# Low-rank inputs of an RWKV-7/attention layer projected with the attention's keys and values (one core)

## The chip, the core and the metric

One core of a Trainium2 chip runs the whole program in one launch. The metric is device time in microseconds. Engines: TensorE (PE; its weight loads are the rows PEld), VectorE (DVE), ScalarE (ACT), GpSimd (POOL) and SyncE (SP, which here only issues DMAs). They run side by side and meet through semaphores; each goes through its own instructions in order.

## What is computed

One layer on x (2048 tokens, width 1024, float32). The part that matters:

```python
h = modulate(rms_norm(x, norm1_g), sh1, sc1)
proj = h @ w_in                       # columns: r 512, k 512, v 512, low rank 32+32+96, q 512, k 128, v 128
feat = proj[..., :RWKV_COLS]
feat = feat + (prev - feat) * shift_mix          # prev: the token before
r, k, v, w_lo, a_lo, g_lo = split(feat)
w = -softplus(-(w0 + tanh(w_lo) @ w2)) - 0.5     # decay
iclr = sigmoid(a0 + a_lo @ a2)
gate = sigmoid(g_lo) @ g2
# ... the recurrence over (r, decay, k, v, iclr), and beside it
# attention of q over a window of two chunks of 64 tokens, 8 query heads, 2 key/value heads
x = x + gt1 * (concat(y_rwkv, y_att) @ w_out)
x = x + gt2 * hier_moe(...)           # 32 experts, top 2
```

## The kernel before

**Passes.** The first pass (`pass1`) goes through 16 tiles of 128 tokens: input projection, all elementwise work of the RWKV group, and the windowed attention; it writes a pack per tile to memory. A second pass does the recurrence and the output projection, and then come the experts. Only the first pass is changed.

**Order.** Every engine runs the steps of one table, `ORDER`, in its order, each engine those it has a part in. An entry is a name and how many tiles ahead of the current one (t) it works: 0 is the current tile, 1 the next. The table is run once ahead of the loop with only the entries that work ahead, 15 times in full, and once with only the entries of the tile itself. So the projections of tile t+1 stand between the dependent steps of tile t on TensorE.

**Projection steps on TensorE.** `in_group` (matmuls on line 453) makes groups with channels as rows: 128 columns of w_in are the stationary operand, the transposed activations hT (128 tokens) the moving one, 8 matmuls per 128 channels. r, k and v have 4 times 128 channels, each group in two steps (in_r1, in_r2 and so on). The low-rank inputs are two more such pieces, `in_wa` (64 channels) and `in_g` (96 channels), 8 matmuls each. `in_tok` (line 464) makes groups with tokens as rows: hT is stationary and w_in moving, q with 512 columns in two steps of 4 matmuls (in_q1, in_q2), attention's keys and values with 256 columns in one step of 8 (in_kv).

**Other steps of TensorE, in order.** xT (L438) transposes the next tile's x; lora1 (L474, L479, L484) multiplies the low-rank inputs out; ew1 (L491), ew2 (L498), nbc (L504); att2 (L533) transposes normed q and k; att3_0 and att3_1 (L546) are the logits of heads 0 to 3 and 4 to 7; tok1 and tok2 (L516, L523) transpose RWKV features; att4_0 and att4_1 (L560) transpose the probabilities; att5_0 and att5_1 (L573) multiply them with the values.

**Steps on the other engines.** ev_r, ev_k, ev_v, ev_lora: ScalarE copies a group from PSUM (L618; for lora L615 and L616), GpSimd forms the difference to the token before (L720), VectorE mixes (L761). ev_q (L625) and ev_kv (L630) are ScalarE copies. xT on ScalarE (L602) modulates the next tile's activations into hT in 8 instructions. norm: ScalarE's squares (L593), then GpSimd and VectorE. tok1, tok2: ScalarE L663, VectorE L827. att2 on ScalarE: L673, L675. ew3 is VectorE's (L806 to L822). att3: VectorE adds the bias and finds the maximum (L840 to L851). exp_0 and exp_1: ScalarE's exponentials (L683). att4: ScalarE (L695) and VectorE (L861) each copy half of the transposed probabilities.

**PSUM banks.** `USES1` lists for each of the 8 banks its uses in a tile, in order; a use waits until the one before it was read. A0 holds r, v, q; A1 holds k, lora, kv; C3 holds three small things.

The table before, around the change:

```python
("ew3", 0), ("att3_0", 0), ("in_wa", 1),
("tok1", 0), ("exp_0", 0), ("in_g", 1), ("ev_v", 1), ("tok2", 0), ("att3_1", 0), ("exp_1", 0),
("in_q1", 1), ("att4_0", 0), ("in_q2", 1), ("att5_0", 0), ("ev_lora", 1), ("norm", 2),
("att4_1", 0), ("lora0", 1), ("in_kv", 1), ("ev_q", 1), ("att5_1", 0), ("out", 0), ("ev_kv", 1)
```

Of the kernel before, what the change touches and what calls it, by code (L numbers as in the profile page):

```python
# [21 lines left out]
ACT = mybir.ActivationFunctionType  # L22
# [4 lines left out]
P = 128  # L27
NT = T // P
KD = D // P
CHUNK = 64  # L30
HD = 64
C = 512
H = C // HD
CC = C // P
LORA_WA = 64
LORA_G = 96
RW_COLS = 3 * C + LORA_WA + LORA_G
QH, KVH = 8, 2
IN_COLS = RW_COLS + (QH + 2 * KVH) * HD
NF = 3 * CC + 2  # L40
LAMBDA = float(np.exp(-0.5))
NEG = -1e30
KEYS = 192
# [54 lines left out]
def shape_constants():  # L98
# [4 lines left out]
    def put(name, a):  # L103
# [32 lines left out]

USES1 = {"A0": ("r", "v", "q"), "A1": ("k", "lora", "kv"),
         "T0": ("xT", "qT", "tokA", "tokK", "P0", "P1"), "T1": ("xT", "kT", "tokB", "tokV", "P0", "P1"),  # L140
         "C0": ("zw", "nbc", "L0", "L1"), "C1": ("za", "L0", "L1"),
         "C2": ("gate",), "C3": ("ssn", "nT", "bon")}
BANK1 = {b: i for i, b in enumerate(USES1)}
IN_GROUPS = {"r": ("A0", 0), "k": ("A1", 1), "v": ("A0", 2), "lora": ("A1", 3)}


class Sync:
# [224 lines left out]
def pass1(nc, S, ps, V, W, ins, dram, nt):  # L372
    B = Banks(S, "a", USES1, nt, ahead=("xT", "r", "k", "v", "lora", "q", "kv"))
    bank = {b: ps[i] for b, i in BANK1.items()}
# [5 lines left out]
    ORDER = (("xT", 1), ("x", 2), ("lora1", 0), ("kk", 0), ("att1", 0), ("in_r1", 1), ("in_r2", 1), ("ew1", 0),  # L380
             ("in_k1", 1), ("ev_r", 1), ("ew2", 0), ("in_k2", 1), ("nbc", 0), ("att2", 0), ("in_v1", 1), ("in_v2", 1),
             ("ev_k", 1),
             ("ew3", 0), ("att3_0", 0), ("in_wa", 1),
             ("tok1", 0), ("exp_0", 0), ("in_g", 1), ("ev_v", 1), ("tok2", 0), ("att3_1", 0), ("exp_1", 0),
             ("in_q1", 1), ("att4_0", 0), ("in_q2", 1), ("att5_0", 0), ("ev_lora", 1), ("norm", 2),
             ("att4_1", 0), ("lora0", 1), ("in_kv", 1), ("ev_q", 1), ("att5_1", 0), ("out", 0), ("ev_kv", 1))

    def run(eng, steps):

# [11 lines left out]
    with nc.Block() as block:  # L401
        @block.sync
        def _(sp):
            def load_x(n, b):
                if isinstance(n, int) and n >= nt:
                    return
                B.wait_full(sp, "T1", "xT", n - 1)
                sp.dma_start(V["x"], dram["x"][bass.ds(n * P, P), :]).then_inc(S["x"], 16)

            def store(t, b):  # L410
                S.wait(sp, "ya", t + 1)
                sp.sem_inc(S["sp_passed"], 1)
                B.wait_read(sp, "T0", "tokK", t)
                sp.dma_start(dram["mid"][bass.ds(t, 1)].rearrange("a p n -> (a p) n"), V["pk_all"]).then_inc(S["stored"], 16)
                if isinstance(t, int) and t == nt - 2:

                    B.wait_full(sp, "A1", "kv", nt - 1)
                    sp.wait_ge(S["stored"], 16 * (nt - 1))
                    for n in range(2):
                        load_pack(sp, S, W, dram, n, n)  # L420
                    sp.dma_start(W["w_router"], ins["w_router"].rearrange("(k p) n -> p k n", p=P)).then_inc(S["w_out"], 16)
                    sp.dma_start(W["gt1"], ins["gate_b"][:, 0:D].to_broadcast([P, D])).then_inc(S["gate_b"], 16)

            sp.dma_start(dram["xn2"][T:T + 1, :].rearrange("o (a n) -> (o a) n", a=4),
                         V["S"][0:4, :]).then_inc(S["zero_row"], 16)
            run(sp, {"x": load_x, "out": store})
            sp.wait_ge(S["zero_row"], 16)
            sp.wait_ge(S["stored"], 16 * nt)

        @block.tensor  # L430
        def _(pe):
# [9 lines left out]
            def in_group(g, part):  # L441
                name, index = IN_GROUPS[g]

                def go(n, b):
                    if part == 0:
                        B.wait_read(pe, "T1", "xT", n)
                        B.wait_free(pe, name, g, n)
                    parts = [(P * c, P, C * index + P * c) for c in (2 * part, 2 * part + 1)]
                    if g == "lora":
                        parts = [[(0, LORA_WA, 3 * C)], [(P, LORA_G, 3 * C + LORA_WA)]][part]  # L450
                    for at, m, w0 in parts:
                        for kk in range(KD):
                            mm = pe.matmul(bank[name][0:m, at:at + P], V["w_in"][:, kk, w0:w0 + m], V["hT"][:, kk, :],  # L453
                                           start=(kk == 0), stop=(kk == KD - 1))
                    if part == 1:
                        B.full(mm, name)
                return go

            def in_tok(g, name, w0, w, ks=range(KD)):
                def go(n, b):  # L460
                    if ks[0] == 0:
                        B.wait_free(pe, name, g, n)
                    for kk in ks:
                        mm = pe.matmul(bank[name][:, 0:w], V["hT"][:, kk, :], V["w_in"][:, kk, w0:w0 + w],  # L464
                                       start=(kk == 0), stop=(kk == KD - 1))
                    if ks[-1] == KD - 1:
                        B.full(mm, name)
                return go

            def lora1(t, b):  # L470
                S.wait(pe, "lora_in", t + 1)
# [93 lines left out]
            def att5(g):  # L565
                def go(t, b):
                    B.wait_read(pe, "C2", "gate", t)
                    for i in range(4):
# [7 lines left out]
                return go  # L576

            run(pe, {"xT": xT, **{f"in_{g}{part + 1}": in_group(g, part) for g in "rkv" for part in range(2)},
                     "in_wa": in_group("lora", 0), "in_g": in_group("lora", 1),
                     "in_q1": in_tok("q", "A0", RW_COLS, C, range(0, 4)), "in_q2": in_tok("q", "A0", RW_COLS, C, range(4, KD)),  # L580
                     "in_kv": in_tok("kv", "A1", RW_COLS + C, 2 * P), "lora1": lora1, "ew1": ew1, "ew2": ew2, "nbc": nbc,
                     "tok1": tok((("tokA", "T0"), ("tokB", "T1"))), "tok2": tok((("tokK", "T0"), ("tokV", "T1"))),
                     "att2": att2, "att3_0": att3(0), "att3_1": att3(1), "att4_0": att4(0), "att4_1": att4(1),
                     "att5_0": att5(0), "att5_1": att5(1)})
# [2 lines left out]
        def _(act):  # L587
# [7 lines left out]
            def xT(n, b):  # L595
                for half, name in enumerate(("T0", "T1")):
                    B.wait_full(act, name, "xT", n)
                    if half == 0:
                        B.wait_full(act, "A1", "kv", n - 1)
                    for i in range(4):  # L600
                        c = 4 * half + i
                        a = act.activation(V["hT"][:, c, :], bank[name][:, P * i:P * i + P], ACT.Identity,  # L602
                                           scale=V["s1"][:, c:c + 1], bias=V["b1"][:, c:c + 1])
                        if i == 3:
                            B.free(a, name)

            def ev(g):
                name, index = IN_GROUPS[g]

                def go(n, b):  # L610
                    B.wait_full(act, name, g, n)
                    S.wait(act, "feat", 4 * (n - 1) + index + 1)
                    S.wait(act, "hist", 4 * (n - 1) + index + 1)
                    if g == "lora":
                        act.activation(V["raw_v"][0:LORA_WA, 12, 1:P + 1], bank[name][0:LORA_WA, 0:P], ACT.Copy)  # L615
                        a = act.activation(V["raw_v"][0:LORA_G, 13, 1:P + 1], bank[name][0:LORA_G, P:2 * P], ACT.Copy)  # L616
                    else:
                        a = act.activation(V["raw_v"][:, 4 * index:4 * index + 4, 1:P + 1],  # L618
                                           split(bank[name][:, :], 4), ACT.Copy)
                    B.free(a, name)  # L620
                return go

            def ev_q(n, b):
                B.wait_full(act, "A0", "q", n)
# [35 lines left out]
            def tok(use):  # L660
                def go(t, b):
                    B.wait_full(act, "T0", use, t)
                    B.free(act.activation(pk[use[3]], bank["T0"][:, :], ACT.Copy), "T0")  # L663
                return go
# [26 lines left out]
            def att4(g):  # L691
                def go(t, b):
# [3 lines left out]
                return go  # L696

            run(act, {"norm": norm, "xT": xT, "ev_r": ev("r"), "ev_k": ev("k"), "ev_v": ev("v"), "ev_lora": ev("lora"),
                      "ev_q": ev_q, "ev_kv": ev_kv, "lora0": lora1, "kk": kk, "ew1": ew1, "ew2": ew2, "tok1": tok("tokA"),
                      "tok2": tok("tokK"), "att1": att1,  # L700
                      "att2": att2, "exp_0": att3(0), "exp_1": att3(1), "att4_0": att4(0), "att4_1": att4(1)})

# [175 lines left out]
def views(nc, ctx):  # L878
# [3 lines left out]
    V = {}  # L882
# [22 lines left out]
    w_in_at = a.at  # L905
    V["w_in"] = split(a.take(KD * IN_COLS), KD)
    V["w_in_at"] = (w_in_at, a.at)
    for name, w in (("raw", NF * (P + 1)), ("qkv0", 768), ("qkv1", 768), ("Pb", 8 * 65), ("kT", 2 * KEYS), ("Pm", 1024)):
        V[name] = a.take(w)
    V["raw_v"], V["kT_v"], V["Pm_v"] = split(V["raw"], NF), split(V["kT"], 2), split(V["Pm"], 4)  # L910
    V["Pb_v"] = split(V["Pb"], 8)
# [1144 lines left out]
    return np.concatenate([up, down], 1).reshape(NE * PIECES, P, PIECE)  # L2056


def host_arrays(inputs):

    a = {n: np.asarray(v) for n, v in inputs.items()}
# [10 lines left out]
    for name, src in (("c", "c"), ("ada_b", "ada_b"), ("n1g", "norm1_g"), ("n2g", "norm2_g"), ("w0", "rwkv_w0"),  # L2072
# [5 lines left out]
    consts, onehot = shape_constants()  # L2078
    return {"x": a["x"].reshape(T, D), "cols": cols, "rows": rows, "consts": consts, "onehot": onehot,
            "gate_b": np.concatenate([b[2], b[5]])[None, :],  # L2080
            "ada": a["ada_w"][0].reshape(KD, P, 12, 512).transpose(2, 1, 0, 3).reshape(12, P, KD * 512), "w_in": a["w_in"][0], "w2": a["rwkv_w2"][0], "a2": a["rwkv_a2"][0],
            "g2": a["rwkv_g2"][0], "rel_bias": a["rel_bias"], "w_out": a["w_out"][0],
            "w_router": np.concatenate([a["router_grp_w"][0], a["router_exp_w"][0]], 1),
            "wex": expert_pieces(a["exp_w1"][0], a["exp_w3"][0], a["exp_w2"][0])}
# [13 lines left out]
```

## Time and profile before

| | |
|---|---|
| median of 3 runs | 2824.12 us (2823.98 to 2825.91) |
| the profiled execution | 2824.7 us, its span 2822.8 us |
| granted TensorE clock, mean | 0.937 of full |
| busy, share of the span | TensorE 88%, VectorE 38%, ScalarE 27%, GpSimd 15% |
| costliest group of the first pass | L453, TensorE matmuls, 3584 instructions, 419.2 us busy |
| the same for L464 | 512 instructions, 174.3 us busy |

The span runs from the first to the last instruction; the time beside it is the whole execution. Instructions of TensorE overlap, so a row's own length says more than the time it takes from the stream; that is read from start to start. A note in square brackets behind a row is idle time before it and what ended it.

### The profile page before, as it was taken

The page shows a single profiled execution, that of the slowest core. Times are in us where ns is not written, and L with a number is a line of the kernel's source. Part 1 is how long each engine was busy: PE and PEld are TensorE (multiplying, and loading weights), DVE is VectorE, ACT ScalarE, POOL GpSimd, SP SyncE. Part 2 cuts the span into 40 slices and gives each one's busy share as a digit, 9 for nine tenths or more (in the row PEclk, how much of TensorE's full clock was granted, in tenths as well). Part 3 has the DMA queues.
Part 4 walks back from the last instruction along what each step waited for, and adds up shares of the span by engine and source line. Part 5 has one row for each costly group of instructions (what it writes and reads, how often), then busy time and mean ns, then how long its engine had stood idle before and what let it go on. Part 6 is the DMA issues. An engine that isn't in the chain of part 4 may idle for free. (4 is left out here: it accounts for less than half of the span.)

```text
span 2822.8 us, 68456 instructions
## 1 busy us (share of the span) xinstructions
PE 2487.4 (88%) x28334; PEld 1608.1 (57%) x28335; DVE 1067.1 (38%) x2595; ACT 752.7 (27%) x1799; POOL 418.2 (15%) x497
## 2 busy tenths in 40 slices
PE   3999999999998789999999996479999999999940
PEld 2888888888887567777767674223332333232210
DVE  0344544544545245556555654411111111111108
ACT  0244344343343112232323231012222222221112
POOL 0212212212112012121212120000010101000000
PEclk8999999999998799999999997589999999999975
DMA  8012111111123732222222221565535396999959
GB/s 323 9 55 82 46 64 72 46 74 63 46 83 122 275 124 84 100 85 99 85 99 89 95 85 38 226 273 223 215 141 215 141 371 242 380 388 380 365 233 362
DMA packets 55113, 458.35 MB, mean 162 GB/s; under 512 B 7981, under 2 KB 9041, under 8 KB 32625
## 3 DMA queue, kind: packets, MB, share of 16 engines
q1 hardware_dynamic: 39240, 405.59, 36.7%
q0 software_dynamic: 10656, 38.80, 3.6%
q10 hardware_dynamic: 5000, 10.80, 1.1%
q8 instruction: 170, 2.79, 0.4%
q14 instruction: 47, 0.38, 0.0%
HBM read 367.61 MB, written 87.56 MB: 161 GB/s over the span
## 5 line engine op out<-in xcount | busy, mean ns | idle before, releaser
L1742 PE MATMUL ps<-arena 128*32 128x512 f32 x4608 | 513.4, 602 | 29.4 <-DMA arena<-wex 29.4
L453 PE MATMUL ps<-arena 128*128 128x128 f32 (+2 forms) x3584 | 419.2, 276 | 2.1 <-ACT arena L602 2.1
L453 PEld LDWEIGHTS ps<-arena 128*128 128x128 f32 (+2 forms) x3584 | 406.4, 186 | 16.9 <-ACT arena L602 12.9
L1742 PEld LDWEIGHTS ps<-arena 128*32 128x32 f32 x4608 | 150.4, 111 | 385.7 <-issue 362.7
L1100 PE MATMUL ps<-arena 64*64 64x64 f32 x8704 | 299.2, 222 | 30.0 <-ACT arena L1303 9.4
L1100 PEld LDWEIGHTS ps<-arena 64*64 64x64 f32 x8704 | 279.5, 137 | 58.4 <-issue 56.6
L1756 PE MATMUL ps<-arena 128*32 128x512 f32 x2304 | 267.3, 605 | 14.4 <-DMA arena<-wex 13.6
L1245 PE MATMUL ps<-arena 128*128 128x512 f32 x512 | 238.7, 610 | 0.7 <-ACT arena L1322 0.7
L1962 DVE TENSOR_TENSOR arena<-arena,ps 128x256 f32<-128x256 f32 x72 | 29.9, 416 | 464.9 <-ACT arena L1800 464.9
L1800 ACT ACT_TABLE_LOAD x36 | 46.2, 1283 | 595.1 <-PE ps L1742 595.1
L464 PE MATMUL ps<-arena 128*128 128x256 f32 (+1 forms) x512 | 174.3, 488 | 0.0
L1756 PEld LDWEIGHTS ps<-arena 128*32 128x32 f32 x2304 | 68.6, 111 | 159.3 <-issue 147.2
L1245 PEld LDWEIGHTS ps<-arena 128*128 128x128 f32 x512 | 92.9, 191 | 101.9 <-issue 97.7
L761 DVE SCALAR_TENSOR_TENSOR arena<-arena 128x128 f32<-128x128 f32 (+1 forms) x224 | 64.6, 348 | 209.2 <-POOL arena L720 209.2
L1303 ACT ACTIVATE arena<-ps 128x512 f32<-128x512 f32 (+1 forms) x160 | 89.2, 557 | 182.1 <-PE ps L1100 181.0
L1785 ACT ACTIVATE arena<-ps,arena 128x128 f32<-128x128 f32 x296 | 107.5, 468 | 103.1 <-PE ps L1723 103.1
L464 PEld LDWEIGHTS ps<-arena 128*128 128x128 f32 x512 | 93.2, 189 | 56.4 <-issue 50.4
L720 POOL TENSOR_TENSOR arena<-arena 128x512 f32<-128x512 f32 x64 | 59.8, 934 | 403.6 <-ACT arena L618 289.9
L1970 DVE COPY arena<-ps 128x512 f32<-128x512 f32 x72 | 46.4, 686 | 176.7 <-PE ps L1756 176.7
L1402 DVE TENSOR_TENSOR arena<-ps,arena 128x256 f32<-128x256 f32 x160 | 68.2, 426 | 116.6 <-PE ps L1100 114.5
L1359 POOL TENSOR_TENSOR arena<-arena 128x256 f32<-128x256 f32 x32 | 23.3, 729 | 502.2 <-DVE arena L1394 502.2
L683 ACT ACTIVATE arena<-arena 128x192 f32<-128x192 f32 x128 | 56.6, 443 | 103.1 <-DVE arena L851 103.1
(326 smaller groups left out, 3009.7 us busy)
## 6 DMA issues: line engine op xcount, KB each, us to landing
arena<-wex SPq DMA_DIRECT2D x105, 2048.0 KB, 10.1
mid<-arena SPq DMA_DIRECT2D x16, 2568.0 KB, 8.5
arena<-mid SPq DMA_DIRECT2D x16, 2568.0 KB, 9.8
arena<-ada SPq DMA_DIRECT2D x12, 2048.0 KB, 9.6
arena<-x SPq DMA_DIRECT2D x47, 512.0 KB, 9.4
arena<-y SPq DMA_DIRECT2D x16, 1024.0 KB, 8.3
arena<-w_in SPq DMA_DIRECT2D x8, 1232.0 KB, 25.4
x<-arena SPq DMA_DIRECT2D x16, 512.0 KB, 2.7
```

Source lines behind the costliest of these rows:

```text
L453: mm = pe.matmul(bank[name][0:m, at:at + P], V["w_in"][:, kk, w0:w0 + m], V["hT"][:, kk, :], start=(kk == 0), stop=(kk == KD - 1))
L464: mm = pe.matmul(bank[name][:, 0:w], V["hT"][:, kk, :], V["w_in"][:, kk, w0:w0 + w], start=(kk == 0), stop=(kk == KD - 1))
L683: act.activation(V["Pm_v"][:, i, 64:256], V["L"][:, i, :], ACT.Exp, bias=V["negm"][:, h:h + 1], accum_out=V["sm"][:, h:h + 1])
L720: pool.tensor_tensor(V["delta"][0:m, 0:c1 - c0, :], raw[0:m, c0:c1, 0:P], raw[0:m, c0:c1, 1:P + 1], ALU.subtract).then_inc(S["delta"], 1)
L761: i = dve.scalar_tensor_tensor(V["f"][b][0:m, c, :], V["delta"][0:m, c - c0, :], col("mix")[0:m, c:c + 1], V["raw_v"][0:m, c, 1:P + 1], AL ...
L1100: mm = pe.matmul(bank[name][rows, at + CHUNK * i:at + CHUNK * i + CHUNK], lhs(rows, h), rhs(rows, h), start=True, stop=True)
L1245: mm = pe.matmul(bank[name][:, :], W["yT"][:, kk, :], W["w_out"][:, kk, 512 * n0:512 * n0 + 512], start=(kk == 0), stop=(kk == KD - 1))
L1303: B.free(act.activation(XX[:, g, o:, :], split(bank[f"X{g}"][:, 256 * o:], 2 - o), ACT.Copy), f"X{g}")
L1402: B.free(dve.tensor_tensor(Z[:, 4 * g:4 * g + 4, :], split(bank[f"Z{g}"][:, 0:256], 4), k("ident64").unsqueeze(1).to_broadcast([P, 4, CHUN ...
L1742: mm = pe.matmul(bank[("HA", "HB")[g]][rows[j], :], xT[:, kk, rows[j]], slot[j][:, at:at + 2 * FH], start=(kk == 0), stop=(kk == KD - 1))
L1756: mm = pe.matmul(bank[f"Y{n0}"][rows[j], :], hT[:, c, rows[j]], slot[j][:, at:at + 512], start=(c == 0), stop=(c == 3))
L1785: a = act.activation(xT[:, c, :], bank[f"X{c // 4}"][:, P * (c % 4):P * (c % 4) + P], ACT.Identity, scale=V["s2"][:, c:c + 1], bias=V["b2" ...
```

## The change

The low-rank inputs leave `in_group`. Their 160 columns of w_in are moved behind those of the attention's keys and values (on the host, `in_columns`), and the kv group becomes 416 columns wide, tokens as rows, in two steps of 4 matmuls (in_kv1, in_kv2), which take the places of in_wa and in_g. A new ScalarE step, ev_l, copies the 160 low-rank columns from bank A1 into a new buffer `lt` (128 tokens as rows); a new TensorE step, turn_l, transposes them (64 and 96 wide) into bank C3, which gets a fourth use; ev_lora reads there. q is done in three steps: 4, 2 and 2 matmuls (in_q1, in_q2, in_q3), the last in in_kv's place. ev_q moves behind att5_1, next to ev_kv. The waits that guarded w_in and hT by in_kv, the last projection, now name q.

```diff
-USES1 = {"A0": ("r", "v", "q"), "A1": ("k", "lora", "kv"),
+USES1 = {"A0": ("r", "v", "q"), "A1": ("k", "kv"),
...
-         "C2": ("gate",), "C3": ("ssn", "nT", "bon")}
+         "C2": ("gate",), "C3": ("ssn", "nT", "bon", "lora")}
...
-             ("ew3", 0), ("att3_0", 0), ("in_wa", 1),
-             ("tok1", 0), ("exp_0", 0), ("in_g", 1), ("ev_v", 1), ("tok2", 0), ("att3_1", 0), ("exp_1", 0),
-             ("in_q1", 1), ("att4_0", 0), ("in_q2", 1), ("att5_0", 0), ("ev_lora", 1), ("norm", 2),
-             ("att4_1", 0), ("lora0", 1), ("in_kv", 1), ("ev_q", 1), ("att5_1", 0), ("out", 0), ("ev_kv", 1))
+             ("ew3", 0), ("att3_0", 0), ("in_kv1", 1),
+             ("tok1", 0), ("exp_0", 0), ("in_kv2", 1), ("ev_v", 1), ("tok2", 0), ("att3_1", 0), ("exp_1", 0),
+             ("in_q1", 1), ("ev_l", 1), ("att4_0", 0), ("turn_l", 1), ("in_q2", 1), ("att5_0", 0), ("ev_lora", 1), ("norm", 2),
+             ("att4_1", 0), ("lora0", 1), ("in_q3", 1), ("att5_1", 0), ("out", 0), ("ev_q", 1), ("ev_kv", 1))
...
-                    B.wait_full(sp, "A1", "kv", nt - 1)
+                    B.wait_full(sp, "A0", "q", nt - 1)
...
+            def turn_l(n, b):
+                S.wait(pe, "lt", n + 1)
+                B.wait_free(pe, "C3", "lora", n)
+                pe.transpose(bank["C3"][0:LORA_WA, 0:P], V["lt"][:, 0:LORA_WA], ident)
+                B.full(pe.transpose(bank["C3"][0:LORA_G, P:2 * P], V["lt"][:, LORA_WA:], ident), "C3")
...
-                     "in_wa": in_group("lora", 0), "in_g": in_group("lora", 1),
-                     "in_q1": in_tok("q", "A0", RW_COLS, C, range(0, 4)), "in_q2": in_tok("q", "A0", RW_COLS, C, range(4, KD)),
-                     "in_kv": in_tok("kv", "A1", RW_COLS + C, 2 * P), "lora1": lora1, "ew1": ew1, "ew2": ew2, "nbc": nbc,
+                     "in_q1": in_tok("q", "A0", Q_AT, C, range(0, 4)), "in_q2": in_tok("q", "A0", Q_AT, C, range(4, 6)),
+                     "in_q3": in_tok("q", "A0", Q_AT, C, range(6, KD)), "in_kv1": in_tok("kv", "A1", KV_AT, KV_COLS, range(0, 4)),
+                     "in_kv2": in_tok("kv", "A1", KV_AT, KV_COLS, range(4, KD)), "turn_l": turn_l, "lora1": lora1, "ew1": ew1, "ew2": ew2, "nbc": nbc,
...
-                        B.wait_full(act, "A1", "kv", n - 1)
+                        B.wait_full(act, "A0", "q", n - 1)
...
+            def ev_l(n, b):
+                B.wait_full(act, "A1", "kv", n)
+                B.wait_full(act, "C3", "lora", n - 1)
+                act.activation(V["lt"], bank["A1"][:, 2 * P:KV_COLS], ACT.Copy).then_inc(S["lt"], 1)
```

## Rows read from the trace of the kernel before

**Rows 1.** The profile page, part 1: busy time, share of the span, instructions.

```profile
PE 2487.4 (88%) x28334; PEld 1608.1 (57%) x28335; DVE 1067.1 (38%) x2595; ACT 752.7 (27%) x1799; POOL 418.2 (15%) x497
```

**Rows 2.** Busy time by stretch, first pass: us per engine (instructions), then granted clock.

```profile
300.00:400.00 100.00, 99.38 (x759) 87.48 (x758) 47.77 (x114) 41.44 (x108) 20.00 (x22) 1.00 0.17 64
```

**Rows 3.** Line 573 on TensorE: idle time before it, times, and its releaser.

```profile
  ACT arena L695: 8.9, 16
```

**Rows 4.** Timeline of TensorE, one tile: start us, us, line, [idle before, releaser].

```profile
491.36 0.87 PE L533 MATMUL ps<-arena 128*128 128x128 f32 x6
...
499.31 0.92 PE L546 MATMUL ps<-arena 64*128 64x192 f32 x8
500.17 1.97 PE L453 MATMUL ps<-arena 128*64 128x128 f32 x16
502.07 1.09 PE L516 MATMUL ps<-arena 128*128 128x128 f32 x8
503.00 1.92 PE L453 MATMUL ps<-arena 128*96 128x128 f32 x16
504.77 1.08 PE L516 MATMUL ps<-arena 128*128 128x128 f32 x8
...
507.42 3.70 PE L464 MATMUL ps<-arena 128*128 128x512 f32 x8
510.96 1.03 PE L560 MATMUL ps<-arena 128*128 128x128 f32 x8
511.83 3.60 PE L464 MATMUL ps<-arena 128*128 128x512 f32 x8
515.74 1.97 PE L573 MATMUL ps<-arena 128*128 128x64 f32 x16 [0.31 <-ACT arena L695]
517.55 1.04 PE L560 MATMUL ps<-arena 128*128 128x128 f32 x8
518.43 3.62 PE L464 MATMUL ps<-arena 128*128 128x256 f32 x16
521.88 1.89 PE L573 MATMUL ps<-arena 128*128 128x64 f32 x16
```

**Rows 5.** Timeline of ScalarE, the same tile and the start of the next.

```profile
502.77 0.60 ACT L663 ACTIVATE arena<-ps 128x512 f32<-128x512 f32 x1 [9.35 <-PE ps L516]
504.58 0.45 ACT L683 ACTIVATE arena<-arena 128x192 f32<-128x192 f32 x1 [1.21 <-DVE arena L851]
...
506.44 0.58 ACT L618 ACTIVATE arena<-ps 128x512 f32<-128x512 f32 x1
...
512.72 0.46 ACT L683 ACTIVATE arena<-arena 128x192 f32<-128x192 f32 x1 [5.22 <-DVE arena L851]
...
515.00 0.60 ACT L695 ACTIVATE arena<-ps 128x512 f32<-128x512 f32 x1
...
515.65 0.26 ACT L616 ACTIVATE arena<-ps 96x128 f32<-96x128 f32 x1
...
518.19 0.60 ACT L695 ACTIVATE arena<-ps 128x512 f32<-128x512 f32 x1 [1.24 <-PE ps L560]
...
523.87 0.38 ACT L630 ACTIVATE arena<-ps 128x256 f32<-128x256 f32 x1 [2.80 <-PE ps L573]
...
544.48 0.60 ACT L673 ACTIVATE arena<-ps 128x512 f32<-128x512 f32 x1 [2.65 <-PE ps L533]
```

**Rows 6.** Timeline of VectorE, the same tile.

```profile
508.17 1.14 DVE L761 SCALAR_TENSOR_TENSOR arena<-arena 128x128 f32<-128x128 f32 x4 [3.03 <-POOL arena L720]
...
509.90 1.01 DVE L840 SCALAR_TENSOR_TENSOR arena<-ps,arena 128x384 f32<-128x384 f32 x2
```

**Rows 7.** Timeline of ScalarE, the tile ahead of the loop.

```profile
104.08 0.39 ACT L630 ACTIVATE arena<-ps 128x256 f32<-128x256 f32 x1 [2.86 <-PE ps L464]
```

**Rows 8.** Busy time by stretch, last tile of the first pass.

```profile
895.00:900.00 5.00, 0.90 (x5) 0.81 (x4) 2.91 (x7) 1.51 (x6) 2.73 (x2) 0.50 0.77 329
```

**Rows 9.** Busy time by stretch, second pass.

```profile
1400.00:1500.00 100.00, 97.43 (x1972) 75.82 (x1972) 58.06 (x157) 27.88 (x62) 19.23 (x18) 1.00 0.27 97
```

More of the change, by code:

```diff
@@ L37 @@
 RW_COLS = 3 * C + LORA_WA + LORA_G
+LORA = LORA_WA + LORA_G
+KV_COLS = 2 * HD * 2 + LORA
 QH, KVH = 8, 2
 IN_COLS = RW_COLS + (QH + 2 * KVH) * HD
+Q_AT, KV_AT = 3 * C, 3 * C + QH * HD
 NF = 3 * CC + 2
@@ L135, in shape_constants @@
     return k, (np.arange(32)[:, None] == by_rel[None]).astype(np.float32)
-USES1 = {"A0": ("r", "v", "q"), "A1": ("k", "lora", "kv"),
+USES1 = {"A0": ("r", "v", "q"), "A1": ("k", "kv"),
          "T0": ("xT", "qT", "tokA", "tokK", "P0", "P1"), "T1": ("xT", "kT", "tokB", "tokV", "P0", "P1"),
          "C0": ("zw", "nbc", "L0", "L1"), "C1": ("za", "L0", "L1"),
-         "C2": ("gate",), "C3": ("ssn", "nT", "bon")}
+         "C2": ("gate",), "C3": ("ssn", "nT", "bon", "lora")}
 BANK1 = {b: i for i, b in enumerate(USES1)}
-IN_GROUPS = {"r": ("A0", 0), "k": ("A1", 1), "v": ("A0", 2), "lora": ("A1", 3)}
+IN_GROUPS = {"r": ("A0", 0), "k": ("A1", 1), "v": ("A0", 2), "lora": ("C3", 3)}
 class Sync:
@@ L448, in go @@
                     parts = [(P * c, P, C * index + P * c) for c in (2 * part, 2 * part + 1)]
-                    if g == "lora":
-                        parts = [[(0, LORA_WA, 3 * C)], [(P, LORA_G, 3 * C + LORA_WA)]][part]
                     for at, m, w0 in parts:
@@ L698, in _ @@
             run(act, {"norm": norm, "xT": xT, "ev_r": ev("r"), "ev_k": ev("k"), "ev_v": ev("v"), "ev_lora": ev("lora"),
-                      "ev_q": ev_q, "ev_kv": ev_kv, "lora0": lora1, "kk": kk, "ew1": ew1, "ew2": ew2, "tok1": tok("tokA"),
+                      "ev_l": ev_l, "ev_q": ev_q, "ev_kv": ev_kv, "lora0": lora1, "kk": kk, "ew1": ew1, "ew2": ew2, "tok1": tok("tokA"),
                       "tok2": tok("tokK"), "att1": att1,
@@ L907, in views @@
     V["w_in_at"] = (w_in_at, a.at)
-    for name, w in (("raw", NF * (P + 1)), ("qkv0", 768), ("qkv1", 768), ("Pb", 8 * 65), ("kT", 2 * KEYS), ("Pm", 1024)):
+    for name, w in (("lt", LORA), ("raw", NF * (P + 1)), ("qkv0", 768), ("qkv1", 768), ("Pb", 8 * 65), ("kT", 2 * KEYS), ("Pm", 1024)):
         V[name] = a.take(w)
@@ L2056, in expert_pieces, with in_columns @@
     return np.concatenate([up, down], 1).reshape(NE * PIECES, P, PIECE)
+def in_columns(w):
+    return np.concatenate([w[:, :3 * C], w[:, RW_COLS:], w[:, 3 * C:RW_COLS]], 1)
 def host_arrays(inputs):
@@ L2080, in host_arrays @@
             "gate_b": np.concatenate([b[2], b[5]])[None, :],
-            "ada": a["ada_w"][0].reshape(KD, P, 12, 512).transpose(2, 1, 0, 3).reshape(12, P, KD * 512), "w_in": a["w_in"][0], "w2": a["rwkv_w2"][0], "a2": a["rwkv_a2"][0],
+            "ada": a["ada_w"][0].reshape(KD, P, 12, 512).transpose(2, 1, 0, 3).reshape(12, P, KD * 512), "w_in": in_columns(a["w_in"][0]), "w2": a["rwkv_w2"][0], "a2": a["rwkv_a2"][0],
             "g2": a["rwkv_g2"][0], "rel_bias": a["rel_bias"], "w_out": a["w_out"][0],
```

## The prediction

> **What bounds the kernel now.** The page first: TensorE is busy 88% of the span [rows 1]. In the stretch of the first pass it is busy 99.4% at the full granted clock, and VectorE, ScalarE and GpSimd are each under half busy [rows 2]. That reads as "TensorE's work is the time", and it is only half true. L573 waits for the ScalarE copy L695 16 times, 8.9 us in all [rows 3]; the timeline of TensorE shows one such wait, of 0.31 us, in a middle tile [rows 4]; 15 of them are 4.7 us, and the rest falls to the last tile, where no projection covers anything. A wait that small and that regular is the sign of two paths of almost equal length, so I followed the other one back.
>
> It runs like this [rows 4 to 6]. TensorE starts att2 (L533) at 491.36. ScalarE copies qT (the same step of the next tile is the row at 544.48, which waited 2.65 us for L533), copies kT, evicts k (L618), GpSimd forms the difference, VectorE mixes and runs ew3, then att3_0; that frees exp_0 on ScalarE at 504.58, which had waited for VectorE. Behind exp_0 ScalarE evicts v (506.44), GpSimd and VectorE (L761, 508.17, which waited for GpSimd) follow, VectorE's att3_1 starts at 509.90, and exp_1 starts at 512.72 after 5.22 us of waiting for L851. Only then is ScalarE free: L695 at 515.00 to 515.60, and TensorE's att5_0 at 515.74. No step of this chain after att2 waits for TensorE. So from att2 to att5_0 the tile takes 24.38 us by this chain (491.36 to 515.74) and TensorE's own work there is 0.31 us shorter; from att5_0 round to the next att2 TensorE sets the pace alone. A period is **chain (att2 to the end of exp_1 and the first thing released behind it) plus TensorE's work from there to the next att2**.
>
> **The change, part by part.** The profiled execution took 2824.7 us with a span of 2822.8; the median of the runs is 2824.12, 0.6 below it, so I add differences to the median.
>
> *TensorE's work.* A float32 matmul is two instructions here, a transpose one. Start to start: 16 of 128 columns take 1.90 (in_wa, 500.17 to 502.07) and 1.77 (in_g); 16 of 256 take 3.45 (in_kv, 518.43 to 521.88), 0.216 each; 8 of 512 take 3.54 (in_q1), 0.4425 each [rows 4]. Between the last two a straight line gives 0.3575 for 416 columns, so the joined projection costs 16 x 0.3575 = 5.72. The transposes at L516 take 0.93 for 8, 0.116 each (502.07 to 503.00), so turn_l costs 0.23. Work: 5.72 + 0.23 - 1.90 - 1.77 - 3.45 = **-1.17 us a tile**. The columns streamed fall because 16 x 160 replace two times 16 x 128.
>
> *Where that work stood.* Much of it moves to in front of the chain's end. New starts, with att3_0 left at 499.31 to 500.17: in_kv1 to 503.03, tok1 to 503.96, in_kv2 to 506.82, tok2 and att3_1 (together 2.65: 504.77 to 507.42) to 509.47, in_q1 to 513.01, att4_0 (0.87) to 513.88. There turn_l waits for ev_l. ev_l is queued on ScalarE behind exp_1, so it starts where L695 starts now, 515.00. It copies 128x160 out of PSUM: bounds 0.26 (L616, 96x128) and 0.60 (L695, 128x512) [rows 5]; a line through L695 and L630 (256 columns, 0.38) gives 0.30, which I take. It ends at 515.30; with the 0.14 that separate L695's end from L573's start, turn_l begins at 515.44. **TensorE stands idle for 513.88 to 515.44, about 1.55 us, where it stood 0.31.** in_q2, four matmuls that used to cover this wait, is now queued behind it.
>
> *From there on.* Before: att5_0 at 515.74, then att4_1, in_kv 3.45, att5_1. After: turn_l 0.23, half of in_q2 (4 x 0.4425 = 1.77), att5_0 and att4_1 unchanged, in_q3 1.77, att5_1. The start of the stretch comes 0.30 earlier (515.44 for 515.74); its length grows by 0.23 + 1.77 + 1.77 - 3.45 = 0.32. Sum: **+0.02 us a tile**. One more satisfied wait stands between the release and turn_l's first instruction (bank C3); its price shows nowhere: bounds 0 and 0.1 (all of L695's end to L573's start is 0.14), taken as 0.03. So +0.05, over 15 full tiles +0.75.
>
> *The other queues.* ScalarE: ev_l adds 0.2 to 0.3 us, and L695 for att5_0 slips from 515.00 to 515.2; att5_0 now asks for it only at 517.44, so it costs nothing. ev_lora waits for turn_l (L616 near 516.05 instead of 515.65); norm and the low-rank activations follow 0.4 later, and the next tile, which reads them, begins only after att5_1 (521.88). Before att5_1 the cover shrinks from in_kv's 3.45 to in_q3's 1.77: the copy L695 starts 0.64 after att4_1 does (518.19 against 517.55) and takes 0.60, so ready at +1.4 with the 0.14, while TensorE arrives at 0.88 + 1.77 = 2.65. Hidden, with 1.2 to spare. ev_q (0.6) falls into att5_1; ScalarE today waits 2.80 us for that end (L630, 523.87), so it fits. VectorE and GpSimd issue nothing new; their lora step starts 0.4 later, in a part of the tile where nothing of the chain is on them. SP only changes which bank it waits for at the end, and in_q3 ends where in_kv ended; no DMA is added, and w_in has the same bytes.
>
> *Two thin margins, costed at nothing.* tok1 and att3_1 come 0.96 and 2.05 later. tok1's first copy (L663, 502.77, 0.60 long) slips to 503.73 to 504.33; exp_0 is released at 504.58, so 0.25 is left. att3_1's first bank is full near 509.26 + 0.2; VectorE asks at 509.90. If the covers were gone, both would push the chain one for one.
>
> *The first tile ahead of the loop* has no chain: it saves 1.17, but ev_q now stands between the last matmul and ev_kv, which starts right after it today (L630, 104.08 [rows 7]); one copy of 0.60 (L695's length, the same shape) is exposed. Net -0.6. The last tile has no projections: 0.
>
> Sum: +0.75 - 0.6 = +0.15. Forecast **2824 us**, no change. Its own bounds: ev_l between 0.26 and 0.38 (-0.04 to +0.08), turn_l and the restart behind a wait between -0.1 and +0.1 (the 0.14 of today's restart either way, rounded), the extra wait 0 to 0.1: -0.15 to +0.25 a tile, so 2821 to 2828. About 0.2% (5.6 us) is what a measurement of this kernel tells from no change; it would take 0.37 us a tile.
>
> **Rivals.**
> *A, the work comes through.* If ScalarE were free when turn_l arrives, the period would fall by all 1.17: 16 x 1.17 = 19, so 2805. For it: TensorE 99.4% busy. Against: exp_1 cannot start before 512.72 and holds ScalarE to 515.00, ahead of ev_l in program order. The row shows 0.216 for 256 columns and 0.4425 for 512, in proportion, so width in itself buys nothing here and only the fewer columns do. The Trainium skill (Perfetto Trace Analysis, Optimizing Tensor Performance, Matmuls) holds that larger matmuls are more efficient than smaller ones; by that rule the gain would be this rival's or more, and the trace agrees only on the work, not on the wait. A partial form, in which some of the chain slackens, would give 2812 to 2818. Chance of both 0.11.
> *B, slower: the wide matmul is late for the chain.* Place: in_kv1 and in_kv2 ahead of tok1 and att3_1. If an instruction of 416 columns takes as long as one of 512, in_kv1 and in_kv2 take 7.08 together; exp_0 slips by 0.43 and att3_1's banks fill at about 510.83, 0.93 past 509.90. The chain is gated by TensorE again, +0.93 a tile, x15 = +14: 2838. It decides from 0.385 a piece on. Against: the straight line through 256 and 512. Smaller forms (ev_l near 0.60: +0.3 a tile, 2829 with the other terms) lie between. Chance 0.13.
> *C, the clock falls.* In the drained last tile of the pass TensorE was busy 0.90 of 5.00 us and the clock was 0.50 [rows 8]; a stretch of the second pass with 2.6 us idle in 100 kept 1.00 [rows 9], and this change makes it some 3 in 100. If each wait of 1.55 us halved the clock over the 5.8 us of turn_l to att4_1, that would be +5.8 a tile, 2911. The Trainium skill (TensorE: Matmul & The Clock Gate, Part 1) says that an idle TensorE falls back to half rate; no row here shows that for a gap this short. Chance 0.01.
>
> **Chances.** The forecast case 0.75, A 0.11, B 0.13, C 0.01. The forecast's own range lies inside 0.2%, but margins I have not seen may take 0.02 of it to faster and 0.03 to slower. Some of B's small forms stay within. Faster 0.13, same 0.71, slower 0.16. The range reaches from the small forms of A to those of B: 2817 to 2830.5.
>
> **What would show it.** The idle before turn_l's transposes, released by ScalarE's ev_l, near 1.5 us, 15 times, and the 0.31 before L573 gone; in_kv1 plus in_kv2 near 5.7 us; exp_1 still about 21.4 us behind att2's start; the period still 52.4 us. A TensorE that reaches turn_l later than ScalarE would prove the chain wrong and A right; exp_0 or att3_1 released by TensorE would prove B.

## The result, and the profile after

The changed kernel takes 2859.7 us (median of 4 runs, 2857.88 to 2860.55) against 2824.05 us before: ratio 1.0129, 95% interval 1.0116 to 1.0142, slower by 35.6 us. That is outside the forecast range. The profiled execution has a span of 2858.7 us.

Page of the changed kernel: part 1, then two lines of part 2, whose slices are 71 us each.

```profile
PE 2482.0 (87%) x27854; PEld 1560.3 (55%) x27855; DVE 1069.3 (37%) x2595; ACT 758.1 (27%) x1815; POOL 417.4 (15%) x497
...
PE   3999999999999589999999998379999999999940
...
PEclk6999999999999689999999998579999999999975
```

The answer to [rows 1] is that TensorE is busy 5 us less than before, in a span 36 us longer. So the loss is not added work. It is idle time, and work done at a lower clock, as the stretches show; the columns are those of [rows 2].

Busy time by stretch, changed kernel:

```profile
300.00:400.00 100.00, 94.53 (x661) 77.31 (x660) 43.20 (x105) 44.59 (x120) 18.32 (x21) 0.98 0.17 64
532.00:534.00 2.00, 0.13 (x1) 0.14 (x2) 0.00 (x0) 1.88 (x10) 0.00 (x0) 0.80 0.00 0
534.00:536.00 2.00, 2.00 (x4) 0.96 (x4) 0.31 (x2) 1.76 (x5) 0.80 (x2) 0.50 0.00 0
538.00:540.00 2.00, 2.00 (x19) 1.98 (x19) 0.01 (x1) 0.45 (x1) 0.00 (x0) 1.00 0.00 0
```

TensorE's share fell from 99.4% to 94.5%, and its mean granted clock from 1.00 to 0.98. Inside one tile, the stretch of idling is followed by one at a granted clock of 0.50, and 4 us later it is 1.00 again.

Timeline of TensorE, the same kind of tile as in [rows 4]:

```profile
508.58 0.87 PE L540 MATMUL ps<-arena 128*128 128x128 f32 x6
...
517.38 3.06 PE L465 MATMUL ps<-arena 128*128 128x416 f32 x8
520.28 1.04 PE L523 MATMUL ps<-arena 128*128 128x128 f32 x8
521.15 2.96 PE L465 MATMUL ps<-arena 128*128 128x416 f32 x8
523.95 1.04 PE L523 MATMUL ps<-arena 128*128 128x128 f32 x8
...
530.10 1.04 PE L567 MATMUL ps<-arena 128*128 128x128 f32 x8
533.87 0.42 PE L474 MATMUL ps<-arena 128*64 128x128 f32 x1 [2.73 <-ACT arena L633]
...
534.29 3.05 PE L465 MATMUL ps<-arena 128*128 128x512 f32 x4
537.18 1.89 PE L580 MATMUL ps<-arena 128*128 128x64 f32 x16
...
539.79 1.88 PE L465 MATMUL ps<-arena 128*128 128x512 f32 x4
541.51 1.89 PE L580 MATMUL ps<-arena 128*128 128x64 f32 x16
```

Line 540 is att2, L465 in_tok, L523 tok, L567 att4, L580 att5, L474 turn_l. The wide steps in_kv1 and in_kv2 take 2.90 and 2.80 us, 5.70 together. Then come 2.73 us of idling before turn_l, and behind it in_q2 takes 2.89, where in_q3, four instructions of the same shape, takes 1.72 (539.79 to 541.51).

Timeline of ScalarE in that tile (L695 is exp, L633 is ev_l):

```profile
521.80 0.46 ACT L695 ACTIVATE arena<-arena 128x192 f32<-128x192 f32 x1 [0.29 <-DVE arena L863]
...
531.23 0.45 ACT L695 ACTIVATE arena<-arena 128x192 f32<-128x192 f32 x1 [6.04 <-PE ps L567]
...
533.51 0.30 ACT L633 ACTIVATE arena<-ps 128x160 f32<-128x160 f32 x1
```

This is the row that answers the one at 512.72 in [rows 5]. Before, exp_1 was released by VectorE's maximum (L851) and started 21.36 us behind att2. Now it is released by TensorE's L567, which is **att4_0**, and starts 22.65 us behind att2 (508.58). exp_1 overwrites the buffer of probabilities `Pm` that att4_0 transposes for the heads of exp_0, and waits for it in the code (`B.wait_full(act, "T1", "P1" if g == 0 else "P0", t - 1 + g)`). Line 695's own list of releasers has it 15 times in 16 tiles:

```profile
  PE ps L567: 90.7, 15
  DVE arena L863: 9.0, 17
```

From att2 to att2 the loop took 52.4 us in 12 of 14 intervals before, and 52.7 and 52.8 in the other two. After, 4 of 14 intervals are 53.5 to 53.7 and the other 10 are 54.8 or more; the mean of all 14 is 54.73. (The interval into the last tile, which has no projections, is left out of these counts.)

### The profile page after: what moved, and what is told of

It reads as the page before. It is cut to its first block and busy times, and to the rows that moved or that the text cites. A ratio compares the mean times of both kernels' runs of the same rounds, so it can differ in the third digit from the quotient of the medians.

```text
span 2858.7 us, 67527 instructions
## 1 busy us (share of the span) xinstructions
PE 2482.0 (87%) x27854; PEld 1560.3 (55%) x27855; DVE 1069.3 (37%) x2595; ACT 758.1 (27%) x1815; POOL 417.4 (15%) x497
## 5 line engine op out<-in xcount | busy, mean ns | idle before, releaser
L454 PE MATMUL ps<-arena 128*128 128x128 f32 x3072 | 357.6, 276 | 2.2 <-ACT arena L609 2.1
L454 PEld LDWEIGHTS ps<-arena 128*128 128x128 f32 x3072 | 350.3, 193 | 13.5 <-ACT arena L609 13.2
L465 PE MATMUL ps<-arena 128*128 128x512 f32 (+1 forms) x512 | 230.2, 590 | 0.0
L1257 PEld LDWEIGHTS ps<-arena 128*128 128x128 f32 x512 | 92.8, 191 | 101.9 <-issue 97.7
L465 PEld LDWEIGHTS ps<-arena 128*128 128x128 f32 x512 | 96.1, 200 | 82.7 <-issue 82.7
L695 ACT ACTIVATE arena<-arena 128x192 f32<-128x192 f32 x128 | 56.6, 443 | 99.7 <-PE ps L567 90.7
```

What stands on the lines that cost most here:

```text
L695: act.activation(V["Pm_v"][:, i, 64:256], V["L"][:, i, :], ACT.Exp, bias=V["negm"][:, h:h + 1], accum_out=V["sm"][:, h:h + 1])
L1257: mm = pe.matmul(bank[name][:, :], W["yT"][:, kk, :], W["w_out"][:, kk, 512 * n0:512 * n0 + 512], start=(kk == 0), stop=(kk == KD - 1))
```

## The experiments

My theory had two parts. First, att4_0, put 2 us later by the joined projection, holds exp_1 back, and everything behind exp_1 on ScalarE with it. Second, the longer idle that follows costs a second time, through the clock. The main rival was that the wide matmuls themselves make tok1 and att3_1 late, which the forecast had called a thin margin. The diffs show the core of each variant; the fourth also needs the second buffer in the memory map and zeroed once. The kernel before was timed again beside the variants, with medians of 2825.2 to 2828.2 us, and the ratios are to these. Clock and intervals are of one profiled execution each.

**1. att4_0 ahead of in_q1.**

```diff
-("in_q1", 1), ("ev_l", 1), ("att4_0", 0), ("turn_l", 1), ("in_q2", 1)
+("ev_l", 1), ("att4_0", 0), ("in_q1", 1), ("turn_l", 1), ("in_q2", 1)
```

> The changed kernel with one thing moved: TensorE does att4_0 before in_q1 instead of behind it (ScalarE and VectorE keep their order). Theory (exp_1 on ScalarE overwrites the probabilities that att4_0 transposes, so it waits for att4_0, and late projections hold it back by 1.3 us; then TensorE's idle of 2.7 us before turn_l halves its clock and costs another 1.3 us): exp_1 is released by VectorE (the maximum) again, 21.3 us after att2's start instead of 22.65; the idle before turn_l is 1.3 to 1.6 us. If the clock holds at 1.00 over that idle, the period is 52.2 us and the time about 2820; if it still falls, 53.5 and 2839. Rival (the wide matmuls make tok1 and att3_1 late for exp_0 and the logits): both are as late as before, so the time stays within 3 us of 2860.

2824.57 us, ratio to the kernel before 0.999 (0.9978 to 1.0002). Timelines of TensorE and of ScalarE in this variant:

```profile
489.65 0.88 PE L540 MATMUL ps<-arena 128*128 128x128 f32 x6
...
507.63 1.28 PE L567 MATMUL ps<-arena 128*128 128x128 f32 x8
...
513.64 0.30 PE L474 MATMUL ps<-arena 128*64 128x128 f32 x1 [1.30 <-ACT arena L633]
...
513.89 1.88 PE L465 MATMUL ps<-arena 128*128 128x512 f32 x4
515.61 1.89 PE L580 MATMUL ps<-arena 128*128 128x64 f32 x16
...
541.84 0.88 PE L540 MATMUL ps<-arena 128*128 128x128 f32 x6
```

```profile
511.00 0.45 ACT L695 ACTIVATE arena<-arena 128x192 f32<-128x192 f32 x1 [4.75 <-DVE arena L863]
...
513.28 0.30 ACT L633 ACTIVATE arena<-ps 128x160 f32<-128x160 f32 x1
```

exp_1 is released by VectorE again, 21.35 us behind att2. The idle is 1.30, in_q2 behind it takes 1.72, and the clock held. The period is 52.19 us (489.65 to 541.84). The period is the one expected; the time is 4.6 us above the 2820 that went with it. One move of one step gives back 35 us, so the late tok1 and att3_1, which are as late here as in the changed kernel, cost nothing.

**2. turn_l behind in_q2.**

```diff
-("in_q1", 1), ("ev_l", 1), ("att4_0", 0), ("turn_l", 1), ("in_q2", 1), ("att5_0", 0)
+("in_q1", 1), ("ev_l", 1), ("att4_0", 0), ("in_q2", 1), ("turn_l", 1), ("att5_0", 0)
```

> The changed kernel with turn_l behind in_q2 instead of ahead of it, att4_0 left where it is. Theory: exp_1 is as late as in the changed kernel (22.65 us after att2), but in_q2's 1.77 us now stand inside the wait, which shrinks from 2.7 to about 1.0 us; no clock loss. Period 54.8 - 1.8 - 1.3 = 51.8 us, time about 2818. Rival (ev_l and the transposes themselves cost what was lost): no change, 2860. Rival (late tok1 and att3_1): the loss ahead of the wait stays whole, at best 1.8 us a tile is won, 2833.

2840.7 us, ratio 1.0045 (1.003 to 1.006): better than the change by 19, but 23 short of the expectation. Timeline of TensorE:

```profile
471.70 1.04 PE L567 MATMUL ps<-arena 128*128 128x128 f32 x8
472.58 1.88 PE L465 MATMUL ps<-arena 128*128 128x512 f32 x4
...
521.50 0.30 PE L474 MATMUL ps<-arena 128*64 128x128 f32 x1 [1.01 <-ACT arena L633]
...
522.08 2.06 PE L580 MATMUL ps<-arena 128*128 128x64 f32 x16 [0.17 <-ACT arena L707]
523.93 1.92 PE L567 MATMUL ps<-arena 128*128 128x128 f32 x8
525.64 2.68 PE L465 MATMUL ps<-arena 128*128 128x512 f32 x4
```

Two stretches of the same tile:

```profile
521.50:523.50 2.00, 1.83 (x15) 1.61 (x16) 0.40 (x2) 1.90 (x5) 0.89 (x2) 1.00 0.03 8
524.00:526.00 2.00, 2.00 (x10) 1.98 (x10) 0.87 (x2) 0.97 (x3) 0.42 (x1) 0.50 0.00 0
```

The wait before turn_l is the 1.0 expected. I had missed that att5_0 now stands right behind turn_l and meets the copy L707, which ev_l has pushed back: another 0.17. From turn_l to att5_0 it is 0.58 us where in_q2 came 0.25 behind turn_l in variant 1, so a tile without a loss of clock takes 52.18 us, not 51.8. And the clock did not hold: the first two rows are of a tile where att4_1 takes 0.88 us, and in the next tile it takes 1.71 (523.93 to 525.64). The granted clock was still 1.00 in the 2 us behind the wait and is 0.50 in the stretch from 524. 7 of 14 intervals are 53.8, the others 52.2 to 52.4.

**3. Both moves.**

```diff
-("in_q1", 1), ("ev_l", 1), ("att4_0", 0), ("turn_l", 1), ("in_q2", 1), ("att5_0", 0)
+("ev_l", 1), ("att4_0", 0), ("in_q1", 1), ("in_q2", 1), ("turn_l", 1), ("att5_0", 0)
```

> Both moves: att4_0 before in_q1, turn_l behind in_q2. Theory: ScalarE is through ev_l about 24 us after att2's start and TensorE reaches turn_l at about the same moment, so it hardly waits and all of the saved 1.17 us of work a tile comes through, with the 0.31 wait of the kernel before: period 51.0 us, time 2802 to 2806. If something else in the tile holds TensorE, the period stays above 51.7 and the time above 2813.

2803.4 us, ratio 0.9918 (0.9891 to 0.9945): faster than both kernels. One stretch and the timeline of TensorE:

```profile
400.00:500.00 100.00, 100.00 (x724) 83.42 (x723) 48.12 (x116) 45.01 (x120) 21.29 (x24) 1.00 0.17 64
```

```profile
499.96 5.32 PE L465 MATMUL ps<-arena 128*128 128x512 f32 x12
505.11 0.27 PE L474 MATMUL ps<-arena 128*64 128x128 f32 x1
```

TensorE is busy 100.00 of 100 us. turn_l comes without a wait and the period is 50.87, 1.56 us less than before. The 1.17 us of saved work and the 0.31 us that the kernel before waited are 1.48 of it; the 0.08 left is not traced further.

**4. A second buffer for the probabilities**, the order of steps as changed.

```diff
-B.wait_full(act, "T1", "P1" if g == 0 else "P0", t - 1 + g)
+B.wait_full(act, "T1", "P0" if g == 0 else "P1", t - 1)
...
-act.activation(V["Pm_v"][:, i, 64:256], V["L"][:, i, :], ACT.Exp,
+act.activation(V["Pm_v"][g][:, i, 64:256], V["L"][:, i, :], ACT.Exp,
...
+V["Pm_v"] = [split(V["Pm"], 4), split(V["Pm1"], 4)]
```

> The changed kernel, its order of steps untouched, with a second buffer for the probabilities, so that exp_1 no longer waits for att4_0. Theory: as with att4_0 moved: exp_1 released by VectorE 21.3 us after att2, idle before turn_l 1.3 to 1.6 us, 2820 if the clock holds and 2839 if it falls. Rival (late tok1 and att3_1, or the position of att4_0 as such): unchanged, 2860.

2827.76 us, ratio 1.0003 (0.999 to 1.0017). Timelines of TensorE and ScalarE:

```profile
489.32 0.88 PE L540 MATMUL ps<-arena 128*128 128x128 f32 x6
...
510.84 1.03 PE L567 MATMUL ps<-arena 128*128 128x128 f32 x8
513.30 0.30 PE L474 MATMUL ps<-arena 128*64 128x128 f32 x1 [1.43 <-ACT arena L633]
...
541.51 0.88 PE L540 MATMUL ps<-arena 128*128 128x128 f32 x6
```

```profile
510.67 0.46 ACT L695 ACTIVATE arena<-arena 128x192 f32<-128x192 f32 x1 [4.74 <-DVE arena L863]
```

Here att4_0 starts at 510.84, after exp_1 (510.67), and does no harm. The loss came from the shared buffer and not from att4_0's place as such. The period is 52.19 in this tile too, as expected with the clock held; the median time is 8 us above the 2820 that went with it, and its runs scatter from 2820 to 2833.

**5. The kernel before, att4_0 delayed.** q is split 6 and 2; no work is added.

```diff
-"in_q1": in_tok(..., range(0, 4)), "in_q2": in_tok(..., range(4, KD))
+"in_q1": in_tok(..., range(0, 6)), "in_q2": in_tok(..., range(6, KD))
```

> The kernel before, with q's eight matmuls split 6 and 2 instead of 4 and 4, so that att4_0 starts 1.77 us later and no work is added or taken away. Theory: exp_1 waits for att4_0, so it starts at att4_0's end plus 0.26, 1.1 us later than before (released by TensorE's L560, not by VectorE); TensorE then idles about 1.5 us before att5_0. Period 52.43 + 1.1 = 53.6 us and time 2826 + 17 = 2843 if the clock holds, up to 2862 if it falls in each tile. Rival (the loss belongs to the joined projection or the low-rank transposes): unchanged, 2826.

2852.17 us, ratio 1.01 (1.0072 to 1.0128). Timelines of TensorE (line numbers of the kernel before) and ScalarE:

```profile
504.14 0.88 PE L533 MATMUL ps<-arena 128*128 128x128 f32 x6
...
525.45 1.03 PE L560 MATMUL ps<-arena 128*128 128x128 f32 x8
...
529.60 2.21 PE L573 MATMUL ps<-arena 128*128 128x64 f32 x16 [1.40 <-ACT arena L695]
```

```profile
526.58 0.46 ACT L683 ACTIVATE arena<-arena 128x192 f32<-128x192 f32 x1 [6.31 <-PE ps L560]
```

exp_1 comes 22.44 us behind att2, 1.08 later than before, released by L560. 4 of 14 intervals are 53.5, one is 53.9 and the rest 55.2 or more, between the two ends of the expectation. Without any part of the change, 27 us of loss against 35.6 are here.

**6. The changed kernel with filler ahead of the wait.**

```diff
 def turn_l(n, b):
-    S.wait(pe, "lt", n + 1)
     B.wait_free(pe, "C3", "lora", n)
+    for _ in range(20):
+        pe.transpose(bank["C3"][:, 2 * P:3 * P], ident, ident)
+    S.wait(pe, "lt", n + 1)
```

> The changed kernel with 20 transposes of the identity, 0.11 us each and read by nobody, put in front of the wait of turn_l, so that TensorE works through 2.3 of the 2.73 us it idled; the chain is as it was. Theory (12 to 14 of the 16 tiles lose 1.2 to 1.7 us each to the clock after the wait): no row of turn_l longer than 0.30, period 53.5 us in every tile, time 2860 - 18 + 2.3 for the tile ahead of the loop = 2844, faster by 16 for work added. Rival (all of the loss is the wait): 2860 to 2862.

2841.04 us, ratio 1.0061 (1.004 to 1.0082), against 2859.7 for the change: 20 useless transposes a tile make it 19 us faster. Timeline of TensorE (L474 is the filler, L476 turn_l) and one stretch:

```profile
522.86 2.35 PE L474 MATMUL ps<-arena 128*128 128x128 f32 x20
525.77 0.30 PE L476 MATMUL ps<-arena 128*64 128x128 f32 x1 [0.56 <-ACT arena L635]
```

```profile
400.00:500.00 100.00, 98.89 (x707) 81.77 (x706) 45.97 (x108) 43.70 (x117) 19.97 (x22) 1.00 0.17 64
```

The clock is 1.00, and 13 of 14 intervals are 53.5, the other 53.7. exp_1 is as late as in the change. So 53.5 is the change with its wait and without its clock loss.

**7. Narrow work behind the wait.** As variant 1, but in_q2 is moved behind att4_1, so turn_l is followed by att5_0 and att4_1.

```diff
-("ev_l", 1), ("att4_0", 0), ("in_q1", 1), ("turn_l", 1), ("in_q2", 1), ("att5_0", 0)
+("ev_l", 1), ("att4_0", 0), ("in_q1", 1), ("turn_l", 1), ("att5_0", 0)
...
-("lora0", 1), ("in_q3", 1)
+("lora0", 1), ("in_q2", 1), ("in_q3", 1)
```

> As att4_0 moved ahead of in_q1 (2824.6), but turn_l is followed at once by att5_0 and att4_1 (64 and 128 columns), and in_q2 and in_q3 come together after them. The wait before turn_l stays near 1.3 us; att5_0 now meets the copy L707, which ends about 0.3 us later. If the clock loss with turn_l behind in_q2 came from what stands behind the wait and not from its length, the clock falls here too in part of the tiles and the period alternates between 52.4 and about 54: 2835 to 2850. If length alone decides, the clock holds as with the 1.29 us wait: 52.4, 2828.

2852.47 us, ratio 1.0101 (1.0072 to 1.0129), slightly beyond the upper end of what was expected. Timeline of TensorE:

```profile
525.71 0.30 PE L474 MATMUL ps<-arena 128*64 128x128 f32 x1 [1.30 <-ACT arena L633]
...
526.29 2.09 PE L580 MATMUL ps<-arena 128*128 128x64 f32 x16 [0.17 <-ACT arena L707]
528.17 1.92 PE L567 MATMUL ps<-arena 128*128 128x128 f32 x8
```

The wait before turn_l is the 1.30 of variant 1, where the clock never fell; here 11 of 14 intervals are 54.2 or more. Length alone does not decide. The two variants also differ by the 0.17 that att5_0 waits, so what stands behind the wait and that second gap are not told apart.

**8. The kernel before, att4_0 ahead of in_q1.**

```diff
-("in_q1", 1), ("att4_0", 0), ("in_q2", 1)
+("att4_0", 0), ("in_q1", 1), ("in_q2", 1)
```

> The kernel before with att4_0 ahead of in_q1, nothing else. Theory: before the change att4_0 ended 0.9 us ahead of the maximum that released exp_1, so its wait was covered; moving it earlier gives nothing: period 52.4 us, exp_1 21.4 us after att2, the wait of 0.31 us stays, time as before, 2825. Rival (att4_0's place is worth something of itself, so that the repaired version's gain has little to do with the projection): faster by 5 us or more.

2863.24 us, ratio 1.0118 (1.0098 to 1.0138). Both expectations missed. Timeline of TensorE:

```profile
535.72 0.63 PE L560 MATMUL ps<-arena 128*128 128x128 f32 x4 [0.15 <-ACT arena L663]
538.04 0.84 PE L560 MATMUL ps<-arena 128*128 128x128 f32 x4 [1.69 <-DVE arena L827]
```

Timeline of VectorE in the kernel before, the row between the two of [rows 6]:

```profile
509.23 0.68 DVE L827 COPY arena<-ps 128x512 f32<-128x512 f32 x1
```

In the kernel before, tok2 ends 2 us earlier than in the changed one, but VectorE reads its bank T1 (L827) only after ev_v's mix. att4_0 in its new place runs into that: 1.69 us of waiting for L827 and 0.15 for ScalarE's L663. Its shortest periods, 3 of 14, are 53.94, near 52.43 + 1.84 - 0.31; the other 11 are 55.3 or more. In variant 1 the wide projections had delayed tok2, and the same move cost att4_0 0.25 us there (its row at 507.63 is 1.28 long, 1.03 elsewhere). The early place of att4_0 is good only together with them.

**9. Second buffer and turn_l behind in_q2.**

```diff
 (variant 4, and)
-("att4_0", 0), ("turn_l", 1), ("in_q2", 1), ("att5_0", 0)
+("att4_0", 0), ("in_q2", 1), ("turn_l", 1), ("att5_0", 0)
```

> The changed kernel with the second buffer for the probabilities and turn_l behind in_q2, att4_0 where the change left it. Theory: neither wait is left; TensorE is busy without a gap and the period is 50.9 us as with both moves, 2803 to 2806. If the order of att4_0 matters beyond the wait for its buffer, the period is above 51.5.

2805.72 us, ratio 0.9924 (0.9904 to 0.9945), all intervals but one 50.88 to 50.90. It agrees with variant 3 by the other way.

## Why the prediction was wrong, step by step

**The step that failed** is the sentence "No step of this chain after att2 waits for TensorE". It was true of the releasers in the rows that the forecast followed and false of the code. There exp_1 waits for the maximum and for att4_0, besides its turn on ScalarE, and the trace names only the one that comes last. att4_0 ended at 511.83, 0.9 us ahead of exp_1 at 512.72, and the forecast itself moved that end to 513.88, past it, without asking who waits for att4_0. With the 0.26 from att4_0's end to exp_1 (530.97 to 531.23) the forecast's own numbers give 1.4 us of delay. Measured, exp_1 comes 1.29 us later, and ev_l and turn_l with it. The remaining terms of the sum should have been added to that: variants 1 and 4, without this wait, run at 52.19 a tile, where the forecast's sum gives 52.48. Their 2824.6 and 2827.8 us lie closer to the forecast 2824 than the periods account for: 0.24 us less in 15 tiles would be 3.6 us below the kernel before.

**The sizes.** Forecast against measured, per tile: in_kv1 and in_kv2 5.72, measured 5.70. turn_l 0.23, measured 0.24 at full clock (513.64 to 513.89, variant 1). ev_l 0.30, measured 0.30. Saved work 1.17: variant 3 shows that and 0.08 more. From ev_l's end to turn_l the 0.14 was 0.06 (533.81 to 533.87), each half of in_q 1.72 instead of 1.77, and att5_0 behind turn_l 1.73 where it was 1.81 behind its own wait. These make the period of variant 1 -0.24 instead of +0.05.

**The idle before turn_l** was forecast at 1.55 and was 2.73 us. In variant 4 it is 1.43, in variant 1 1.30, where att4_0's wait for its bank takes part of it.

**Rival A** (the work comes through) did not happen in the change. Variant 3 shows that all of it was there to be had, two moves away. The Trainium skill holds that larger matmuls are more efficient (Perfetto Trace Analysis, Optimizing Tensor Performance, Matmuls). The joined projection does not show it: 416 columns take 0.356 us an instruction and 256 took 0.216, in proportion.

**Rival B** had the right sign and the wrong place. The straight line through 256 and 512 columns held, and both thin margins held: exp_0 is still released by VectorE (0.29 at 521.80), 13.22 us behind att2 as before. The step held back by TensorE was exp_1.

**Rival C** was given 1 chance in 100 because the wait was sized at 1.55 us and because "no row here shows that for a gap this short". It is half of the loss. The Trainium skill (TensorE: Matmul & The Clock Gate, Part 1) says that an idle TensorE falls back to half rate; the trace agrees, with 0.50 in the stretch behind the idle. The price I wrote, 5.8 us for a fall over all of turn_l to att4_1, was wrong twice. The steps it names add up to 4.7 in the forecast's own terms (0.23, 1.77, 1.81 and 0.88). And the fall covers only part of them: 9 of the 10 longer intervals lose 1.3 to 1.7, the first one 3.3.

**The account.** The wait: 53.5 - 52.43 = 1.07 a tile (exp_1's 1.29 later, less the 0.24 above), 15 tiles, 16 us. The clock: 54.73 - 53.5 = 1.23, times 15, 18 us. Together 34 of the 35.6 measured; the two traces, from the first att2 to the last, differ by 34.3. Variant 6, which takes the second part away, is 18.7 faster than the change, and 18.6 by the same stretch of its trace.

## What to carry to other kernels

When a step is moved later, look in the code for everything that waits for it, buffer reuse above all: a wait that is met with 0.9 us to spare has no row in the trace, and it binds once the step is more than that late. Compare every new end time in the sum with the start of each waiter, also where the trace names another releaser. A place in the order is good only relative to its neighbours: the same move of att4_0 won 35 us in one kernel and lost 35 in the other.

## What the runs showed of the hardware

TensorE's clock can halve behind gaps of 1 to 3 us in a stream that is otherwise full, and the length of the gap does not order the cases. Gaps of 1.43 and 1.30 us followed by 512-column matmuls never cost a long period (variants 4 and 1). Gaps of 1.0 to 1.4 us followed by 64-column matmuls did, in 7 (variant 2), 9 (variant 5) and 11 (variant 7) of 14 intervals. But 512-column matmuls behind the gap are no protection: the 2.73 us gap of the changed kernel, followed by them, cost a long period in 10 intervals, and the 1.69 us gap of variant 8, with four transposes and then 512-column matmuls behind it, in 11. What decides between them stays open.

The fall need not lie in the gap. In the changed kernel's tile above the clock is already down when turn_l starts; in variant 2 it was still 1.00 in the 2 us behind the gap and fell while TensorE was busy again. In most cases a tile with a fall is 1.3 to 1.7 us longer, and up to 3.6 in single ones (57.1 against 53.5, variant 5). Twenty useless transposes that filled most of the 2.73 us gap avoided it in all intervals (variant 6).
